# One residual add moved from VectorE to GpSimd at the end of layer 0

## The reference

```python
for l in range(DEPTH):                       # DEPTH = 2
    ...
    h = rms_norm(x, norm_gains[l, 2]) * (1.0 + sc2) + sh2
    y = swiglu(h, w_gate_up[l], w_down[l])
    x = x + g2 * rms_norm(y, norm_gains[l, 3])
# rms_norm(y, g) = y * rsqrt(mean(y * y) + 1e-6) * g
```

## Time and profile before

| | |
|---|---|
| Median of three runs | 2398.86 us |
| The profiled execution's own time | 2399.79 us |
| Its span | 2398.0 us |
| TensorE busy | 2336.8 us, 97% of the span |
| VectorE busy | 1624.9 us, 68% |
| ScalarE busy | 979.8 us, 41% |
| GpSimd busy | 290.2 us, 12% |
| Mean clock granted to TensorE | 0.991 of full |

### The profile page before, as it was taken

One profiled execution on the slowest core, in us unless ns is written; L12 is line 12 of the kernel. 1 busy time (PEld: TensorE's weight loads), 2 busy tenths in 40 slices (PEclk: granted clock), 3 DMA queues, 4 the chain that ended last, 5 costly groups with the idle time before them and its releaser, 6 DMA issues.

```text
span 2398.0 us, 30615 instructions
## 1 busy us (share of the span) xinstructions
PE 2336.8 (97%) x11394; PEld 1885.4 (79%) x11394; DVE 1624.9 (68%) x2718; ACT 979.8 (41%) x1870; POOL 290.2 (12%) x356
## 2 busy tenths in 40 slices
PE   7999999999999999999989999999999999999997
PEld 6778777788788888888768887777888888888885
DVE  6775577667877777576762556776687777655766
ACT  5312355644333333344763225555543333324453
POOL 0526300021000000220120010000200000003001
PEclk8999999999999999999999999999999999999999
DMA  7977301131555464673431111102324554227434
GB/s 287 331 248 207 101 27 27 36 123 62 155 180 174 167 202 134 177 216 97 128 122 48 36 36 45 27 27 80 114 71 167 184 198 171 82 68 237 146 105 148
DMA packets 210755, 311.29 MB, mean 130 GB/s; under 512 B 13063, under 2 KB 145080, under 8 KB 206640
## 3 DMA queue, kind: packets, MB, share of 16 engines
q1 hardware_dynamic: 182688, 205.50, 26.6%
q0 software_dynamic: 27920, 103.84, 13.1%
HBM read 243.48 MB, written 71.02 MB: 131 GB/s over the span
## 4 chain that ended last, share of the span: by engine, by line
PE 86%; DVE 7%; issue 2%; ACT 2%; DMA 1%; POOL 1%; SPq 0%; ACTq 0%; DVEq 0%; POOLq 0%
PE ps L3050 32%; PE ps L3089 15%; PE ps L2580 7%; PE ps L2582 7%; PE ps L2581 7%; PE ps L2930 6%; PE ps L2876 3%; PE ps L2907 3%; DVE F L1836 2%; PE ps L2895 1%; DVE ast L1929 1%; DMA F<-in_w_mod 1%; PE ps L2858 1%; PE ps L2644 1%; DVE wsp L1691 1%
## 5 line engine op out<-in xcount | busy, mean ns | idle before, releaser
L3050 PE MATMUL ps<-hT,wsp 128*128 128x512 f32 x1440 | 333.5, 389 | 2.6 <-issue 2.6
L3050 PEld LDWEIGHTS ps<-hT,wsp 128*128 128x128 f32 x1440 | 269.9, 188 | 60.0 <-issue 4.0
L2580 PE MATMUL ps<-hT,wsp 128*128 128x512 f32 (+1 forms) x744 | 310.2, 417 | 5.0 <-DVE F L2000 5.0
L2582 PE MATMUL ps<-hT,wsp 128*128 128x512 f32 (+1 forms) x744 | 292.5, 393 | 0.0
L2581 PE MATMUL ps<-hT,wsp 128*128 128x512 f32 (+1 forms) x744 | 291.4, 392 | 0.0
L3089 PE MATMUL ps<-wsp,asp 128*128 128x512 f32 x1056 | 249.7, 392 | 0.2
L3089 PEld LDWEIGHTS ps<-wsp,asp 128*128 128x128 f32 x1056 | 198.1, 188 | 44.0 <-issue 1.0
L3050 PE MATMUL ps<-tsum,wasp 128*128 128x512 f32 x960 | 226.4, 392 | 0.0
L3050 PEld LDWEIGHTS ps<-tsum,wasp 128*128 128x128 f32 x960 | 180.2, 188 | 39.5 <-DVE wasp L2376 0.3
L2580 PEld LDWEIGHTS ps<-hT,wsp 128*128 128x128 f32 x744 | 141.9, 191 | 36.3 <-issue 13.2
L2582 PEld LDWEIGHTS ps<-hT,wsp 128*128 128x128 f32 x744 | 141.4, 190 | 31.0
(11 more groups left out here) (296 smaller groups left out, 4285.2 us busy)
## 6 DMA issues: line engine op xcount, KB each, us to landing
F<-in_w_mod SPq DMA_DIRECT2D x80, 512.0 KB, 5.8
raw<-in_w_in SPq DMA_DIRECT2D x48, 512.0 KB, 3.9
raw<-in_w_gate_up SPq DMA_DIRECT2D x48, 512.0 KB, 4.8
raw<-sums_d SPq DMA_DIRECT2D x88, 256.0 KB, 3.1
F<-in_w_gate_up SPq DMA_DIRECT2D x40, 512.0 KB, 5.6
acts_d<-F POOLq DMA_DIRECT2D x38, 512.0 KB, 6.7
F<-acts_d POOLq DMA_DIRECT2D x76, 256.0 KB, 4.3
raw<-in_w_down SPq DMA_DIRECT2D x66, 256.0 KB, 4.0
```

Source lines behind the costliest of these rows:

```text
L2580: mm(o, a(0), b(0), start=start, stop=False)
L2582: return mm(o, a(1), b(0), start=False, stop=stop)
L3050: last = mm(bank(j, p), block_of(p, z)[:, k * P:k * P + P], times(p, zz, k), start=p < B_A22 and k == 0 and z == 0 and zz == 0, stop=k == ...
```

## The change

For layer 0 alone (`l + 1 < L`, with L = 2), `y_sum` of tiles 0 to 5 is left out of VectorE's list, and GpSimd does the same add, with the same operands and shapes, between its `y_root` and its `store`. It waits for `y_mul` (`s_yu`) and for the fetched x (`s_xr`), as `y_sum` did, and counts `s_xs` up. Tiles 6 and 7 stay on VectorE, and before the add of tile 6 VectorE waits until GpSimd has done that of tile 5, so that `s_xs` is counted in order. Layer 1 is unchanged.

```diff
@@ GpSimd
                 for t in range(6):
                     y_root(l, 1, t)
+                    if l + 1 < L:
+                        pool.wait_ge(s_yu, 1 + yj(l, 1, t) + 1)
+                        pool.wait_ge(s_xr[t % 3], uses(l, 1, t) + 16)
+                        nc.gpsimd.tensor_tensor(kn(xt[t % 3]), kn(xt[t % 3]), y_rows(t), ALU.add
+                                                ).then_inc(s_xs, 1)
                     store(l, 1, t)
                     if 1 <= t:
                         fetch(l, 1, t + 2)
@@ VectorE, in the loop over steps
                     for t, b in enumerate(FIRST_BEAT):
                         if e == b + 1:
                             y_mul(1, t)
-                            y_sum(1, t)
+                            if l + 1 == L:
+                                y_sum(1, t)
@@ VectorE, after the loop
                     y_mul(1, 6)
+                    dve.wait_ge(s_xs, yj(l, 1, 5) + 1)
                     y_sum(1, 6)
```

## The result

Seven runs of each kernel: the median goes from 2398.94 us (2397.3 to 2401.5) to 2406.9 us (2403.78 to 2409.67). The ratio is 1.0034 [1.0024, 1.0043], which is 8.2 us more, 5.8 to 10.3. The change makes the kernel slower, by 0.34%. The forecast was 2403.6 us, in a range from 2400.0 to 2408.5. The sign and the range hold, but the loss is 1.7 times the central sum of 4.75 us. The time that rival (a) gave, 2407.4 us, is nearer.

The account below looks back on a forecast made before the run. TensorE was taken as the bound, busy for 97% of the span, with waits fed by VectorE and ScalarE. Per-tile terms summed to 4.75 us; 2398.86 + 4.75 = 2403.6 us, range 2400.0 to 2408.5.

Parts of the forecast that it names:

- central sum of 4.75 us: Predicted total loss over tiles 0 to 5: 0 + 0.4 + 0.9 + 0.9 + 1.35 + 1.2 us.
- rival (a): VectorE's queue goes first and GpSimd's add waits for the whole run behind `y_mul`: 8.5 us, 2407.4 us; chance 0.24.
- Contention for reads: While VectorE or GpSimd reads two SBUF operands the other stands still; a 512-column add holds something for 1.08 us.
- (b): The port is met little, tiles 1 to 3 gain, tiles 4 and 5 lose: about +2 us, 2400.9; chance 0.15.
- (c): Wide add under 1.7 us without blocking, shorter TensorE waits and no slow stretch: -3.1, 2395.8 us; chance 0.05.
- Who goes first: Behind `y_mul`, GpSimd's add reads after one `acts_lo` and holds off `down_lo`, 0.9 us late at tile 2.
- Tiles 0, 1 and 5: Tile 0 costs zero, tile 1 passes 0.4 us into TensorE's wait of 0.27, tile 5's chain costs 1.2 us.
- Tiles 2 and 3: A late `down_lo` behind `y_mul` delays the TensorE steps waiting for it, 0.9 us at each tile.
- first four terms: Predicted losses at tiles 0 to 3: 0 + 0.4 + 0.9 + 0.9 us.
- Tile 4: The late sum passes in full through ScalarE's square, mean and root to `y_mul` of tile 5: 1.35 us.
- (d): Added TensorE idle time brings one more low-clock stretch, +1.66 us, 2405.3; chance 0.53 together with the likeliest case.
- likeliest case: GpSimd's add takes 2.35 us and blocks VectorE's `down_lo`: 2403.6 us, own range 2402.2 to 2406.2; 0.53 with (d).

Follow-up runs that it names:

- gap behind `acts_lo`: Changed kernel plus a one-column VectorE memset directly behind the first `acts_lo` after `y_mul`, ahead of `down_lo`; ratio 1.0011.
- gap behind `down_lo`: Changed kernel plus a one-column VectorE memset behind the first `down_lo` after `y_mul`; ratio 1.0020.
- tile 4 alone: Against the kernel before, only tile 4's add moves to GpSimd, the others stay on VectorE; ratio 1.0014.
- room for the root: Kernel before, with `norm_v` ahead of the sum of tile 7 and ScalarE scaling tile 6 before squaring tile 7; ratio 0.9996.
- spare adds: Kernel before, VectorE keeping its adds, plus two unused 512-column GpSimd adds from SBUF behind `y_mul` of tiles 0 to 5; ratio 1.0035.

## Why the prediction was right, and where it was not

- **The add's own cost.** 2.35 us was predicted, undisturbed ones take 2.36 to 2.41. Right, and the strided y is no dearer. The Trainium skill's GPSIMD Engine Reference (section on performance versus the Vector engine), halved, gave 2.25 us as an estimate; the traces are 0.11 to 0.16 us above it.
- **Contention for reads.** Right in kind: an instruction with two SBUF operands on one engine stands while the other reads, and it isn't a matter of writes, nor of an operand in PSUM. (b) and (c) fall with that. The sum of (c) was wrong in itself, too: it took 1.3 us off a wait of 0.80.
- **Who goes first: the step that failed.** The prediction had the add of tile 2 "ready at 1183.6", that it "begins to read at 1183.8", after the one `acts_lo`, and holds off `down_lo`. In the changed kernel it waits for the whole unbroken row, as in rival (a). The sums come 1.2, 2.2, 1.9, 3.4, 2.8 and 1.2 us later after `y_mul`'s end than before (2.48, 3.46, 3.20, 4.66, 4.04, 2.43 us against 1.27), where the terms had 1.2, 1.5, 1.3, 1.3, 1.35 and 1.2. The test named for it decided: `down_lo` keeps 0.69 us and an add takes over 4. Evidence against (a), that at 83.31 VectorE stood back for three adds, was one place where the row belonged to GpSimd; it spoke for unbroken rows as much as for turns. (a) in turn had 2.3 us of waiting at tile 1, where the add got in ahead of `norm_lo` and waited 1.0.
- **Tiles 0, 1 and 5.** At tile 0 VectorE was blocked for 2.1 us, and TensorE did not notice it: 0, right. Tile 1's 0.4 us on the wait of 0.27 came out as 0.3 (0.59), though the sum was 2.2 us late and not 1.5. At tile 5 the lateness of 1.2 us is right; what it costs no ratio can tell (0.9996), and the stage of that kernel is 1.9 us longer.
- **Tiles 2 and 3.** 0.9 + 0.9 were to come from a late `down_lo`. TensorE's wait of 0.80 us and that of 2.56 are gone instead, because VectorE's queue runs ahead. But the wait of 1.60 is 3.21 us now, for an `acts_lo` and `down_lo` that stood behind ScalarE's late square: the 1 to 2 us of lead that the prediction gave ScalarE there did not cover a sum that came 1.9 us late. Together they cost TensorE nothing up to 1215.13, where it is level with before, and not the 2.2 us that the first four terms make; the lateness reached it behind tile 4.
- **Tile 4: mis-sized.** 1.35 us was predicted, on the chain to tile 5 alone. ScalarE's `acts_hi` stands behind the square that waits 4.18 us for the sum, so TensorE gets a wait that did not exist, 3.91 us. Alone this tile costs 3.4 us (1.2 to 5.5). By the central values no other tile's term is as far off, though the interval still holds 1.35. Rival (a) had the lateness, 1.8 us more at this tile (1.6 measured), but not this customer either.
- **Low clock.** One more stretch at 1.2 GHz was (d), 1.66 us. In the profiled stage it is 3.66 us more, the stretches behind the waits of 3.21 and 3.91 against the one behind 2.56 before. By its size it belongs in the main sum, not beside it. Yet how long a wait is doesn't tell it. Behind 3.39 us, in the kernel with the gap behind `acts_lo`, 12 matmuls take 3.02 us at a granted clock of 1.00. Behind 3.20 us, in the one with the gap behind `down_lo`, the 12 that take 5.49 in the changed kernel take 4.56. And behind the 2.15 us in the kernel with tile 4 alone, 6 take 2.12 for 1.63.
- **ScalarE's wait.** A rise by about 7 us was named, it rose by 12.5 (6.9 to 19.4).

The likeliest case was thus wrong in the one step that told it from (a), and the sum of (a), 8.5 us, came out near the 8.2 measured. That is partly luck, for its parts did not come out as it had them: it let 5.5 of its 7.8 us of lateness reach TensorE and gave nothing to the clock. The sign of the forecast does not hang on the step that failed, since either order makes the kernel slower (the gap behind `acts_lo` builds the predicted one, at 1.0011). The range held because it took in (a): the likeliest case's own ended at 2406.2 (its terms make 2406.1), and the median is 2406.9.

Two things stay open. Why GpSimd's read passed after a single VectorE instruction with the spare adds, and only after two to four in the change, is not settled. The records begin alike, and no run separates the instruction before, the widths and the moment of the request. And the measured 8.2 us exceed the profiled stage's 6.7 by 1.5, which is within the interval. How much of either is the placing of low-clock stretches, single profiles can't tell: at about equal idle time TensorE is busy for 78.28 us before and for 79.30 with the room for the root.

## What to carry to other kernels

Before moving a two-operand SBUF operation from VectorE to GpSimd, list what follows it in VectorE's queue. If that is a row of two-operand reads without a gap, count the add as its own length plus the rest of the row, and then follow every engine that waits for the result, with all that is queued behind its wait. Of the waits that this gives TensorE, one long one can cost more than the same time in pieces, by the low clock behind it (one profile of each kernel shows that, no test by itself). In this kernel GpSimd's memsets and VectorE's `add_out`, with an operand in PSUM, needed no counting.

## What the hardware did that was not expected

- GpSimd's two-operand read waited through 2 to 4 back-to-back VectorE reads (3.12 to 4.58 us for 2.40). A VectorE memset of 0.06 us in between let it in (2.45 us), and then VectorE stood for up to 2.2 us.
- VectorE's busy time hides this, for a blocked instruction counts as busy (2.78 us for 0.69 at tile 0): six adds that had held it for 6.8 us left the stage, and its busy time there fell by 1.7.
- 12 matmuls at a granted clock of 1.00 directly behind 3.39 us of idle time (3.02 us), and 12 at 0.50, 1.2 GHz, behind 3.21 us (5.49 us).
